# Four moving operands of TensorE at unequal distances from its weights

## The reference

```python
def conv_glu_ffn(h, w_up, conv_w, conv_b, w_down):
    z = h @ w_up
    z1 = shift_prev(z)
    z2 = shift_prev(z1)
    z = conv_w[0] * z2 + conv_w[1] * z1 + conv_w[2] * z + conv_b
    gate, val = jnp.split(z, 2, axis=-1)
    return (jax.nn.silu(gate) * val) @ w_down

def swiglu(h, w13, w2):
    a, b = jnp.split(h @ w13, 2, axis=-1)
    return (jax.nn.silu(a) * b) @ w2
```

## Time and profile before

| | |
|---|---|
| median of 3 timed runs | 2422.92 us (2421.53 to 2442.31) |
| profiled execution | 2451.55 us, its span 2449.8 |
| mean granted clock of TensorE | 0.939 |
| busy: TensorE | 94% of the span, 18,344 matmuls |
| busy: weight loads (beside the matmuls) | 90% |
| busy: VectorE, ScalarE, GpSimd | 59%, 48%, 21% |
| DMA | 439 MB, 179 GB/s over the span |

### The profile page before, as it was taken

One profiled execution on the slowest core, in us unless ns is written; L12 is line 12 of the kernel. 1 busy time (PEld: TensorE's weight loads), 2 busy tenths in 40 slices (PEclk: granted clock), 3 DMA queues, 4 the chain that ended last, 5 costly groups with the idle time before them and its releaser, 6 DMA issues.

```text
span 2449.8 us, 46010 instructions
## 1 busy us (share of the span) xinstructions
PE 2304.2 (94%) x18344; PEld 2211.7 (90%) x18344; DVE 1434.1 (59%) x2021; ACT 1164.3 (48%) x1558; POOL 511.3 (21%) x265
## 2 busy tenths in 40 slices
PE   8989999998999899997999999998999999788998
PEld 7879799996999799995999999996899899778998
DVE  4553389955699669775469843365533344355544
ACT  5411265545655534464444444455544444454654
POOL 0022000010000245420044434410144400000443
PEclk9869799999999899996899999998999999889999
DMA  6200168742578368661268655542355355623542
GB/s 243 104 1 1 55 256 307 283 175 87 191 300 311 149 253 342 248 224 54 95 262 323 256 189 188 189 156 92 138 185 182 130 182 185 173 76 119 181 181 103
DMA packets 62223, 439.05 MB, mean 179 GB/s; under 512 B 7228, under 2 KB 7612, under 8 KB 9638
## 3 DMA queue, kind: packets, MB, share of 16 engines
q1 hardware_dynamic: 59472, 430.75, 47.7%
q0 software_dynamic: 976, 2.63, 0.7%
q10 hardware_dynamic: 1670, 4.17, 0.5%
HBM read 434.89 MB, written 2.62 MB: 179 GB/s over the span
## 4 chain that ended last, share of the span: by engine, by line
PE 79%; DVE 8%; ACT 5%; issue 4%; POOL 2%; DMA 1%; DVEq 0%; SPq 0%; ACTq 0%; POOLq 0%
PE ps L276 19%; PE ps L278 19%; PE ps L277 19%; DVE mix L581 2%; PE ps L290 2%; POOL hf L389 2%; PE ps L292 2%; PE ps L298 2%; PE ps L394 1%; ACT w_hi L255 1%; PE ps L405 1%; DVE w_lo L261 1%; PE ps L1379 1%; DMA ring<-in_weights 1%; PE ps L954 1%
## 5 line engine op out<-in xcount | busy, mean ns | idle before, releaser
L276 PE MATMUL ps<-h_hi,w_hi 128*128 128x256 f32 x3512 | 988.5, 281 | 9.5 <-DVE h_lo L2181 4.9
L277 PE MATMUL ps<-h_lo,w_hi 128*128 128x256 f32 x3512 | 985.6, 281 | 0.0
L278 PE MATMUL ps<-h_hi,w_lo 128*128 128x256 f32 x3512 | 985.4, 281 | 0.0
L261 DVE TENSOR_TENSOR w_lo<-ring,w_hi 128x2048 fp32r<-128x2048 f32 x273 | 627.5, 2299 | 549.5 <-ACT w_hi L255 543.9
L255 ACT ACTIVATE w_hi<-ring 128x2048 fp32r<-128x2048 f32 x335 | 640.2, 1912 | 187.9 <-PE ps L278 176.3
L276 PEld LDWEIGHTS ps<-h_hi,w_hi 128*128 128x128 f32 x3512 | 668.0, 190 | 12.8 <-DVE h_lo L2181 5.1
L277 PEld LDWEIGHTS ps<-h_lo,w_hi 128*128 128x128 f32 x3512 | 667.8, 190 | 0.1
L278 PEld LDWEIGHTS ps<-h_hi,w_lo 128*128 128x128 f32 x3512 | 664.8, 189 | 0.0
L276 PE MATMUL ps<-g_hi,w_hi 128*128 (+1 forms) x1232 | 348.2, 283 | 9.8 <-DVE g_lo L711 9.4
L277 PE MATMUL ps<-g_lo,w_hi 128*128 (+1 forms) x1232 | 347.4, 282 | 0.0
L278 PE MATMUL ps<-g_hi,w_lo 128*128 (+1 forms) x1232 | 347.3, 282 | 0.0
(11 more groups left out here) (394 smaller groups left out, 2607.3 us busy)
## 6 DMA issues: line engine op xcount, KB each, us to landing
ring<-in_weights SPq DMA_DIRECT2D x335, 1024.0 KB, 4.8
mix<-in_modw SPq DMA_DIRECT2D x72, 1024.0 KB, 5.0
mix<-in_c_ssd ACTq DMA_DIRECT2D x1, 1536.0 KB, 6.8
bias_rows<-mix POOLq DMA_DIRECT2D x1, 1536.0 KB, 36.2
x<-in_x SPq DMA_DIRECT2D x1, 1024.0 KB, 4.7
mix<-in_c SPq DMA_DIRECT2D x2, 512.0 KB, 5.6
mix<-bias_rows POOLq DMA_DIRECT2D x1, 1024.0 KB, 8.3
out_xT<-hf SPq DMA_DIRECT2D x1, 1024.0 KB, 4.3
```

Source lines behind the costliest of these rows:

```text
L261: dve.tensor_tensor(w_lo[:, n % SLOTS], ring[:, n % SLOTS], w_hi[:, n % SLOTS], ALU.subtract).then_inc(lo_ready[n % SLOTS], 1)
L276: pe.matmul(o, w[0], a_hi, start=first, stop=False, **kw)
L277: pe.matmul(o, w[0], a_lo, start=False, stop=False, **kw)
L278: return pe.matmul(o, w[1], a_hi, start=False, stop=last, **kw)
```

## The change

Four unused tensors are put ahead of `g_hi`, `g_lo`, `h_hi` and `h_lo`. Before, all four started at 192 bytes above a multiple of 512, as the small tensors ahead of them add up to that. After, the offsets from a multiple of 512 are 384 for `g_hi` (192 + 48 x 4), 64 for `g_lo` (another 192), 320 for `h_hi` (192 + 32 x 4) and 256 for `h_lo` (another 112 x 4). Their tiles are 1,024 bytes each, so every tile of a tensor has the offset of the tensor. `e_hi` and `e_lo` stay at 192. `m_ring` and `m_cs` move up by 96 elements, behind the longer region of `g_lo`. All instructions, their order and their waits are the same.

```diff
             acc = over.enter_context(nc.sbuf_tensor("acc", [P, 2, 2, T], F32))
             sil = over.enter_context(nc.sbuf_tensor("sil", [P, 2, T], F32))
             gf = over.enter_context(nc.sbuf_tensor("gf", [P, 2, T], F32))
+            over.enter_context(nc.sbuf_tensor("below_g_hi", [P, 48], F32))
             g_hi = over.enter_context(nc.sbuf_tensor("g_hi", [P, KF, T], F32R))
+            over.enter_context(nc.sbuf_tensor("below_g_lo", [P, 48], F32))
             g_lo = over.enter_context(nc.sbuf_tensor("g_lo", [P, KF, T], F32R))
...
         mix = sb("mix", [P, mixed_size])
+        sb("below_h_hi", [P, 32])
         h_hi = sb("h_hi", [P, KD, T], F32R)
+        sb("below_h_lo", [P, 112])
         h_lo = sb("h_lo", [P, KD, T], F32R)
...
-        m_ring = carve(14336, 2, 2, D)
-        m_cs = carve(18432, D)
+        m_ring = carve(14432, 2, 2, D)
+        m_cs = carve(18528, D)
```

## The result

The change made the kernel slower: the median of four executions is 2467.22 us (2464.76 to 2472.89), against 2426.01 us before (four executions, 2421.53 to 2442.31; one was added to the three of the text ahead). The ratio is 1.0154, with a 95% interval from 1.0107 to 1.02. The forecast was 2391 us, and the time lies 17 us above its range. The profiled executions lie closer together than the medians: 2466.32 us after, one of the four, against 2451.55 before, 14.8 us. The executions of the kernel after spread over 8.1 us, those of before over 20.8.

The account below looks back on a forecast made before the run. TensorE's start-to-start matmul pace was taken as the bound. All slow matmuls turning fast (49 us) gave 2374 or 2402 us by two readings; the middle, 2388, plus a few microseconds for starts after pauses made 2391, range 2368 to 2450.

Parts of the forecast that it names:

- the two paces: L276 to L278 at full clock: the same matmuls follow each other every 113.35 ns or every 117.75, 4.4 ns apart.
- The price of a nanosecond: TensorE's split-weight matmuls, some 15,900: each nanosecond of pace was counted in full in the kernel's time.
- 11,100 x 4.4 ns = 49 us: Upper end of the gain, L276 to L278: every slow matmul becomes fast, 49 us off the profile.
- The two readings of 28.6 us: Profile minus timed median: either profiling's cost (forecast 2374 us) or timed runs already faster in pace (2402); the middle was taken.
- Slow is the rhythm that can be lost: L276 to L278: unequal distances disturb the slow rhythm into the fast one, which stays; favoured case, 2391 us, chance 0.42.
- A distance of 320 alone therefore forbids neither pace: L316 to L318, operand roles exchanged, moving operand at 320: 276 ns in one stretch, 279 in another.
- The loss: Rival, L276 to L278: slow rhythm becomes the rule, 21 us on the profile, timed 2444 to 2472, middle 2458; chance 0.20.
- Nothing changes: Rival: each stretch's start draws its rhythm and distances are no cause; 2422 to 2442 us, likeliest 2424; chance 0.33.
- A better pace than any seen: Rival: matmuls approach the 111 ns of L405's step, up to 38 us more gain, about 2360 us; chance 0.05.
- 281 everywhere, or a pace above 118 ns: Sign of the slower case in the profile after, in the matmuls of L276 to L278.
- only those with `h_*` change: Sign in the profile after: if only g_* or only h_* stages change, distance within a group counts, not the mixture.
- If L276 waits for `w_lo` much beyond 2.7 us: Sign at L276: a faster TensorE has made VectorE's weight split the bound, and part of the gain ends there.

Follow-up runs that it names:

- e4: Not the network: matmul streams with only TensorE working, six pauses per pair of operand distances; at 192 three passes ran at 117.8 ns, three at 113.3.
- e11: e8 with GpSimd instead of VectorE making g_lo and one w_lo of three in ffn0 and ffn1; 2466.46 us, ratio 1.0144 to the kernel before.
- e12: Kernel before with GpSimd instead of VectorE making g_lo and one w_lo of three in ffn0 and ffn1; 2476.4 us, ratio 1.0188.
- e8: Kernel before with all four operands at distance 112 from the weights modulo 512; 2420.05 us, ratio 0.996.
- e6: Kernel before with all four operands at distance 0 from the weights modulo 512; 2481.43 us, ratio 1.0237.
- e13: The kernel before, unchanged, profiled once more; 2429.57 us, pace 114.81 ns.
- e3: Kernel before with only g_hi moved to 384 and g_lo to 64, h_* left at 192; 2430.49 us, ratio 1.0007.
- e9: Kernel before with h_hi and h_lo both moved to 320, g_* left at 192; 2454.94 us, ratio 1.0111.
- e10: Streams with only TensorE working, weights shifted too; at distance 112, 113.3 ns with weights in place, 120.0 with both 16 bytes up.

## Why the prediction was wrong

**The bound, and the two paces: right.** TensorE's pace decides, at 113.35 and 117.75 ns. Both came back in a stream with only TensorE at work (113.3 and 117.8 in e4), and all kernels profiled here but e11 and e12, in which splits were moved between engines, line up by their pace alone. From e8 (113.69 over all operands, 2422.04 us profiled) to e6 (119.94, 2481.25) it is 59.2 us for 6.25 ns, 9.5 us a nanosecond. The eight other profiled executions lie within 7.2 us of this line.

**The price of a nanosecond: a term sized too high.** The sum took 15,900 matmuls x 1 ns = 15.9 us. 9.5 us arrive, 60%. e6 and e8 ran on different chips, beside medians of 2422.17 and 2433.03 us for the kernel before; by their ratios to these, 1.0237 and 0.996, they are 67 us apart, 10.8 us a nanosecond. So the price lies between 0.6 and 0.7 of the pace. "11,100 x 4.4 ns = 49 us" would have been 29 by the first figure, and e8, which is that case, is 29.5 us shorter in profile. The prediction had no term for what comes back in waits, though it named the sign itself: that part of the gain would end where TensorE is fast enough to wait for VectorE.

**The two readings of 28.6 us: the second was right, and should have decided.** The difference between profile and median was pace. The profiled executions of after and e8, 2466.32 and 2422.04 us, are each one of the runs counted and not the slowest, so profiling costs nothing that shows; and e13 shows the kernel before at 2429.57 us with a pace of 114.81. So much of the fast rhythm had probably been drawn already in the timed runs; they left no trace. By the line above, an estimate, the median of 2426 us stands for a pace of about 114.1 (e8's 113.69 and 4 us / 9.5), give or take 0.8 for executions that lie 7 us off the line. The upper end of the gain against the timed runs was then some 7 us (114.1 less 113.35, times 9.5), and not 49 or 21. The prediction took the middle.

**"Slow is the rhythm that can be lost": the step that failed.** It rested on two rows. The settling after the pause at 600.8 us was a start at 192, where the fast rhythm is in the lot; nothing in it says that the rhythm exists elsewhere. And unequal distances did not disturb a slow rhythm into a fast one: they replaced both by others, of 118.8 at (320, 256). Nor is fast the rhythm that stays: in e3 a settled 113.4 turns into 118.8 at the first matmuls on the moved `g_*`, with no pause and no fall of the clock, turn after turn. That the trace before showed no such change was true, and it could not show one, as all operands of `product` lay at one distance. The case for the gain inferred from one distance to four others, with no row of `product` at any of them.

**"A distance of 320 alone therefore forbids neither pace": right as it stands, and of little use.** With `h_*` moving at 320 (e9) both paces occur, but the fast one in 3% of the matmuls on `h_*`, and in the stream at 64 (e4) in none of six passes. So 320 does not forbid the fast pace; it makes it rare, and with 256 beside it none is left. The row for the sentence, L316 to L318 at 276 ns, has the roles exchanged, with the weights moving and `h_*` loaded, and e10 shows why that says little of L276 to L278: where the pair lies counts as well. The kernel after shows this line too, at 290 ns on the mean of all 160 where the earlier trace rows has 283:

```profile
L320 PE MATMUL ps<-w_hi,h_hi 128*128 128x256 f32 x160 | 46.4, 290 | 0.0
```

**The rivals.** The loss had a chance of 0.20 and the right mechanism: the fast rhythm pushed out in every stream of L276 to L278. Of its times, 2444 to 2472, 25 us in 28 lie above 2447, nine tenths and not three quarters, so the chance of slower came out some 0.03 too small. Its price by the second reading was 2472 us timed, which is 5 us from what came; the middle with the first reading, 2458, spoiled it, and the range ended at 2450. Two errors cancel in the 2472: the slow pace is 118.4 over all operands, not 117.75 (the upper end of the loss was "each fast one becomes slow", 21 us, with nothing slower than the slow pace; the first two rows of the table with e8 grow by 30.5 us), and a nanosecond is worth less: profile against profile only 14.8 us of these arrive, inside the stated limit of 21. The rest of the loss is that the timed runs had been faster than the profile. From about 114.1 to 118.37 ns it is 4.3 x 9.5 = 41 us, and the medians are 41 apart (37 by the ratio); this says no more than that the kernel after lies on the line, since the 114.1 was read from it. "Nothing changes" was refuted with its two premises half true: a phase is drawn at the start, and the spread came from it, but the address sets what can be drawn, and how often. The rule of the Trainium skill on independent read ports stood behind this rival, and the runs disagree with it. "A better pace than any seen" did not occur: nothing ran below 113.3 ns at any of more than a hundred combinations of places.

**What was to be seen in the profile after.** "281 everywhere, or a pace above 118 ns" was written there for the slower case, and it is what stands there: 280, 286, 280. The sign "only those with `h_*` change" came true in a form that was not meant: only they cost time. "If L276 waits for `w_lo` much beyond 2.7 us" named the right engine for e8, but the wrong wait: `w_lo` came to 3.1 us there, and `g_lo` to 18.3.

## What to carry to other kernels

Where a profile shows the same instructions at two paces without a wait between, profile two or three more executions first: they tell how often each pace is drawn, and so how much of the gain is still to be had. Measure the pace at a new address in a stream of its own, with pauses, before moving a tensor; it takes one short kernel, and its figures held in the kernel within 0.3 ns. It is no full list of paces, though: with both `h_*` at 320 the kernel had a few fast stretches that the streams had not. And price a faster bound by a slope between two measured versions, since here only 0.6 to 0.7 of each saved nanosecond arrived.

## What was unexpected of the hardware

- The pace of matmuls of 256 columns in fp32r, each with a weight load of its own, depends on where the moving operand lies: 113.3 to 122.3 ns with only TensorE at work, the same again 256 bytes further up. Equal distances of 112 and 368 bytes gave 113.3 in sixteen starts of sixteen, and 4 bytes beside it 120 to 122.
